# A sixth quad in the seven-product form in every MLP block of a two-layer decoder trunk

## What is computed

```python
def squared_relu_mlp(h, w_up, w_down):
    a = jnp.square(jax.nn.relu(h @ w_up))      # (256, 2048) @ (2048, 8192)
    return a @ w_down                          # (256, 8192) @ (8192, 2048)

for layer in range(2):
    x = x + mixer(rmsnorm(x, ln_mix_g[layer])) # attention of two kinds
    x = x + squared_relu_mlp(rmsnorm(x, ln_mlp_g[layer]), w_up[layer], w_down[layer])
```

## Time and profile before

| what | value |
|---|---|
| median of 3 runs | 2080.2 us |
| profiled execution, own time | 2079.74 us |
| its span, first to last instruction | 2078.0 us |
| TensorE busy | 2065.8 us |
| VectorE busy | 1451.2 us |
| ScalarE busy | 1087.7 us |
| granted clock of TensorE | 1.00 throughout |
| one MLP block, of 8 | 172.86 us |

### The profile page before, as it was taken

The page is one execution under the profiler, slowest core; times in us unless marked ns, Lnnn a source line. Parts: engine busy times, 40 slices in busy tenths (PEclk is TensorE's granted clock), DMA queues, the critical chain, the costliest instruction groups (busy, mean ns, idle before and its releaser), DMA issues.

```text
span 2078.0 us, 25877 instructions
## 1 busy us (share of the span) xinstructions
PE 2065.8 (99%) x10386; PEld 1751.5 (84%) x10386; DVE 1451.2 (70%) x1893; ACT 1087.7 (52%) x1553; POOL 85.5 (4%) x133
## 2 busy tenths in 40 slices
PE   8999999999999999999999999999999999999999
PEld 7888888888888888888888898888888888888887
DVE  6545555566966876886697687556886796687787
ACT  6545565445544544554556676444554454454454
POOL 0000000000000000000000255000000000000000
PEclk9999999999999999999999999999999999999999
DMA  8544554655566566565555443455565565656554
GB/s 285 175 151 163 162 162 143 193 174 191 195 199 202 175 225 187 174 223 179 193 193 184 156 127 122 162 182 182 182 223 182 196 204 187 198 184 209 181 182 162
DMA packets 198479, 381.96 MB, mean 184 GB/s; under 512 B 10892, under 2 KB 17112, under 8 KB 198360
## 3 DMA queue, kind: packets, MB, share of 16 engines
q1 hardware_dynamic: 198312, 380.29, 56.4%
q10 hardware_dynamic: 48, 0.02, 0.0%
HBM read 378.19 MB, written 2.10 MB: 183 GB/s over the span
## 4 chain that ended last, share of the span: by engine, by line
PE 98%; DVE 1%; ACT 0%; DMA 0%; issue 0%; POOL 0%; SPq 0%; DVEq 0%; ACTq 0%; POOLq 0%
PE psum L1505 23%; PE psum L1436 14%; PE psum L1438 14%; PE psum L1437 14%; PE psum L1508 11%; PE psum L1726 5%; PE psum L1727 5%; PE psum L1725 5%; PE psum L1569 1%; PE psum L1655 1%; PE psum L1523 1%; DVE halves L988 0%; PE psum L1632 0%; PE psum L1478 0%; PE psum L1656 0%; PE psum L1616 0%
## 5 line engine op out<-in xcount | busy, mean ns | idle before, releaser
L988 DVE TENSOR_TENSOR halves<-raw,halves 128x1024 fp32r<-128x1024 f32 (+1 forms) x724 | 858.0, 1194 | 461.0 <-ACT halves L696 455.9
L696 ACT CAST halves<-raw 128x1024 fp32r<-128x1024 f32 (+1 forms) x724 | 730.3, 1019 | 646.2 <-PE psum L1438 343.7
L1505 PE MATMUL psum<-h,halves 128*128 128x512 f32 x2048 | 639.2, 395 | 0.0
L1508 PEld LDWEIGHTS psum<-h,halves 128*128 128x128 f32 x2048 | 380.3, 188 | 87.4
L1508 PE MATMUL psum<-h,halves 128*128 128x256 f32 x2048 | 398.1, 278 | 0.0
L1436 PE MATMUL psum<-halves,a 128*128 128x512 f32 x828 | 326.3, 394 | 0.0
L1438 PE MATMUL psum<-halves,a 128*128 128x512 f32 x828 | 322.8, 390 | 0.0
L1437 PE MATMUL psum<-halves,a 128*128 128x512 f32 x828 | 322.4, 389 | 0.0
L1505 PEld LDWEIGHTS psum<-h,halves 128*128 128x128 f32 x2048 | 314.4, 189 | 2.8
L1436 PE MATMUL psum<-halves,h 128*128 128x512 f32 (+1 forms) x508 | 202.0, 398 | 0.0
L1438 PE MATMUL psum<-halves,h 128*128 128x512 f32 (+1 forms) x508 | 195.0, 384 | 0.0
(11 more groups left out here) (239 smaller groups left out, 1867.3 us busy)
## 6 DMA issues: line engine op xcount, KB each, us to landing
raw<-in_mlp_w_up SPq DMA_DIRECT2D x128, 1024.0 KB, 5.3
raw<-in_mlp_w_down SPq DMA_DIRECT2D x128, 1024.0 KB, 5.2
raw<-in_sf_w_in SPq DMA_DIRECT2D x45, 1024.0 KB, 5.1
raw<-in_sf_w_o SPq DMA_DIRECT2D x16, 1024.0 KB, 5.1
raw<-in_mla_w_o SPq DMA_DIRECT2D x16, 1024.0 KB, 5.1
raw<-in_mla_w_down SPq DMA_DIRECT2D x8, 1024.0 KB, 5.1
raw<-in_mla_w_ukv SPq DMA_DIRECT2D x8, 1024.0 KB, 5.4
raw<-in_mla_w_uq SPq DMA_DIRECT2D x8, 768.0 KB, 4.6
```

What stands on the lines that cost most here:

```text
L696: nc.scalar.copy(half_piece(n, 0), raw_piece(n)).then_inc(hi_done, 1)
L988: v.tensor_tensor(half_piece(n, 1), raw_piece(n), half_piece(n, 0).bitcast(F32), ALU.subtract)\
L1505: last = mm(bank, half_piece(n, 0)[:, cols], src[:, k].rearrange("p s t -> p (s t)"), start=(k == 0), stop=(k == KT - 1))
L1508: last = mm(bank[:, T:2 * T], half_piece(n, 1)[:, cols], src[:, k, 0], start=False, stop=False)
```

## The change

Quads 0, 1, 3, 4, 6 and 7 take the seven-product form in place of 0, 1, 3, 5 and 7; quads 2 and 5 stay plain. A block has 76 pieces in place of 75. The sixth set of token sums gets a buffer `sd_nat` in the memory of `nat`, which is the work buffer of the up projection; it is made while column 0 of the down projection runs. The places of all weight sums in the order of VectorE are set anew, and the counts in the waits follow (18 and 24 per block in place of 15 and 20).

```diff
-FAST_QUADS = 0, 1, 3, 5, 7
-PLAIN_QUADS = 2, 4, 6
+FAST_QUADS = 0, 1, 3, 4, 6, 7
+PLAIN_QUADS = 2, 5
...
+        with nc.sbuf_tensor("sd_nat", [P, 4, 2, P], F32R) as sd_nat:
+            pass
         nat = sb("nat", [P, 2, TT, N])
...
         def sd_of(i):
-            return sd[:, i] if i < 4 else sd_last[:]
+            return sd[:, i] if i < 4 else (sd_last, sd_nat)[i - 4][:]
...
                 for j in range(32, BLOCK_PIECES):
                     if base + j + AHEAD < P_END:
                         split_hi(base + j + AHEAD)
+                    if j == 34:
+                        token_sums_hi(no, 5)
...
-                sums = {35: 0, 37: 1, quad_at(2) - 3: 2, quad_at(4) - 3: 3, quad_at(6) - 3: 4}
+                sums = {34: 0, 37: 1, quad_at(2) - 3: 2, quad_at(3) - 1: 3, quad_at(5) - 2: 4, quad_at(6) - 1: 5}
...
                     if j == 33:
                         token_sums_lo(no, 4)
+                        token_sums(no, 5)
+                    if j == 35:
+                        token_sums_lo(no, 5)
```

More of the change, by code:

```diff
@@ L147, in all_pieces @@
             for i, (kind, load, half) in enumerate(block_plan(layer, b0)):
-                count = 15 * block_no(layer, b0) + 3 * load + (1 if kind == "t13" else 3) if kind[0] == "t" else 0
+                count = 18 * block_no(layer, b0) + 3 * load + (1 if kind == "t13" else 3) if kind[0] == "t" else 0
                 put(block_base(layer, b0) + i, kind, load, half, count)
@@ L933, in token_sums_hi @@
             def token_sums_hi(no, i):
-                act.wait_ge(a_step, 20 * no + 4 * i + 4)
+                act.wait_ge(a_step, 24 * no + 4 * i + 4)
                 nc.scalar.copy(sd_of(i)[:, :, 0], a_sum).then_inc(sd_hi, 1)
@@ L1274, in weight_sums @@
                 one, two = pair_loads(layer, b0, q // 2)
-                done = 15 * block_no(layer, b0) + 3 * m
+                done = 18 * block_no(layer, b0) + 3 * m
                 for load in (one, two):
@@ L1289, in token_sums @@
             def token_sums(no, i):
-                done = 20 * no + 4 * i
+                done = 24 * no + 4 * i
                 if done:
@@ L1303, in token_sums_lo @@
             def token_sums_lo(no, i):
-                dve.wait_ge(sd_hi, 5 * no + i + 1)
+                dve.wait_ge(sd_hi, 6 * no + i + 1)
                 v.tensor_tensor(sd_of(i)[:, :, 1], a_sum, sd_of(i)[:, :, 0].bitcast(F32), ALU.subtract)                 .then_inc(sd_ready, 1)
@@ L1788, in mlp_block @@
                             if q in FAST_QUADS:
-                                pe.wait_ge(sd_ready, 5 * no + FAST_QUADS.index(q) + 1)
+                                pe.wait_ge(sd_ready, 6 * no + FAST_QUADS.index(q) + 1)
                                 fast_quad(base + quad_at(q), q, added0 + 1)
```

## The result

The kernel after took **2100.97 us** (median of 4 runs, 2100.5 to 2103.26) beside 2080.26 of the kernel before on the same chip: ratio 1.0102, interval 1.0089 to 1.0114. It is slower by 20.7 us, where 15.2 were forecast. 1.0102 on the 2080.2 of the front is 2101.4, just above the range. The sign, the three places and their releasers came out as forecast. What failed is the price of a wait beyond its length: TensorE's start behind its releaser, forecast at 0.05 us, and its restart, forecast at nothing, each once per wait.

The account below looks back on a forecast made before the run. TensorE was taken to set the pace. Three stalls put on 2.58 us per block, the saving takes off 0.68: 1.90 net, 15.2 in eight blocks, so 2095.4 us against the median 2080.2; range 2089 to 2101, likeliest case 2093 to 2100.

Parts of the forecast that it names:

- the three places: TensorE would wait, per block, at the third piece of quad 0 and the first pieces of quads 4 and 7.
- the rival of the full saving: VectorE's average slack, 37 us per block, hides the added work; all 5.4 us show, 2074.8 us; chance 0.05.
- The saving: TensorE's matmuls for one more seven-product quad fall from 24 to 21: 0.68 us per block, 5.4 in all.
- Stall A: Third piece of quad 0 waits for VectorE's additions to x_tok, delayed by the sixth token sums: 0.97 us per block.
- B: First piece of quad 4 waits for VectorE's split, behind weight sums between quads 3 and 4: 0.68 us per block.
- C: First piece of quad 7 waits for VectorE's split, after two sets of weight sums: 0.93 us per block.
- A chain of 5.2: Between quads 3 and 4, TensorE's 4.76 us of work would have to hold a VectorE chain of 5.2.
- Unknown costs ... I take nothing, as that row is the nearest: TensorE's restart behind a 512-column matmul: nothing taken; upper bound 0.16 us per stall, 3.9 us in all.
- each stall costs more than its wait: Rival: twice the 0.16 us restart bound at each of 24 stalls, 7.7 us on top, 2103 us; chance 0.07.
- which changes nothing in this sum: Quad 0's weight sums, moved from j = 35 to 34, stay ahead of the additions: no effect on their delay.
- VectorE is the later one there: ScalarE's casts 39 and 40 are ready before VectorE asks, so ScalarE's added casts cost nothing.
- recorded 0.16 shorter than the loss: TensorE's waits in the profile after would read about 0.8, 0.5 and 0.8 us at the three places.

Follow-up runs that it names:

- work_free: The kernel after without the sixth token sums and the weight sums of quads 4 and 7: 2074.98 us, ratio 0.9974.
- no_token: The kernel after without the sixth token sums and ScalarE's cast of them, all weight sums kept: 2091.46 us, ratio 1.0055.
- no_sums_4: The kernel after without the weight sums of quad 4 alone: 2094.34 us, ratio 1.0068.
- no_sums_4_7: The kernel after without the weight sums of quads 4 and 7, sixth token sums kept: 2084.45 us, ratio 1.0019.
- token_only: The kernel before plus the sixth token sums, made but unused, weight sums of quad 0 still at j = 35: 2094.59 us, ratio 1.0069.
- token_only_34: token_only with the weight sums of quad 0 moved from j = 35 to j = 34: 2089.59 us, ratio 1.0042.
- delay_060: The kernel before plus one useless VectorE operation of 512 elements per block, ahead of the additions to x_tok: 2082.8 us, ratio 1.0014.
- delay_114: The kernel before plus one useless VectorE operation of 1024 elements per block, ahead of the additions to x_tok: 2087.31 us, ratio 1.0033.
- delay_228: The kernel before plus two useless VectorE operations of 1024 elements per block, ahead of the additions to x_tok: 2095.98 us, ratio 1.0073.
- respread: The kernel after with the three operations of each set of weight sums put behind splits of their own: 2084.88 us, ratio 1.0023.
- vector_sums: pool_sums with the weight sums of quads 2 and 3 back on VectorE, those of quads 0 and 1 one split earlier: 2101.81 us, ratio 1.0104.
- pool_sums: The kernel after with fast quads 0, 1, 2, 3, 5, 7, sixth token sums inside the up projection, weight sums of quads 2 and 3 on GpSimd: 2128.38 us, ratio 1.0229.

## Why the prediction was right, and where it was wrong

- **What bounds the kernel**: right. TensorE, with VectorE close behind it in the quads; the average slack of 37 us per block was of no use, although the rival of the full saving counted on it.
- **The saving**, 0.68 us per block: right, shown by work_free.
- **Stall A, B, C**: right in place, releaser and cause, shown by taking the causes away (A in no_token, B in no_sums_4, B and C in no_sums_4_7), and independent of each other. VectorE's lateness was 0.96, 0.64 and 0.94 for 0.92, 0.63 and 0.88. Two readings beside stall B were loose. "A chain of 5.2" is 5.4 by the prediction's own rows (4.76 + 0.68). And the b22 split is not held by piece 49 alone: its cast on ScalarE runs from 714.90 to 715.53, and the split starts at 715.70, directly behind the split before it. So something earlier could have helped, by some 0.13 us. Neither changes the sum.
- **"Unknown costs ... I take nothing, as that row is the nearest"**: this step failed, together with the 0.05 us for TensorE's start taken from the same. Both terms had the right place in the sum and the wrong size. A wait costs 0.15 before the first matmul and 0.08 to 0.12 in the steps behind it, 0.25 together, where I had 0.05: 0.20 x 24 = 4.8 of the 5.7 us that the rows show missing. Neither size was hidden. In the trace of before TensorE waits for another engine in the mixers too, and the earlier trace rows is only one of two kinds of start. The other, behind VectorE:

```profile
1180.45 0.74 DVE L1163 TENSOR_SCALAR mix<-psum,gains 128x512 f32<-128x512 f32 x1
...
1181.31 0.42 PEld L1569 LDWEIGHTS psum<-ident,mix 128*128 128x128 f32 x4 [0.93 <-issue]
1181.34 0.63 PE L1569 MATMUL psum<-ident,mix 128*128 128x128 f32 x4 [0.64 <-DVE mix L1163]
```

1180.45 + 0.74 = 1181.19, the weight load 0.12 behind it, the matmul 0.15. The three stalls wait for VectorE too, so this was the nearer row. The slow step behind a first matmul stands in that trace as well, at 512 columns, though behind small matmuls and not behind a wait:

```profile
177.04 0.47 PE L1436 MATMUL psum<-halves,h 128*128 128x512 f32 x1
177.35 0.39 PE L1437 MATMUL psum<-halves,h 128*128 128x512 f32 x1
```

A record of 0.47 and a step of 0.31, as behind all three stalls; the trace of before has 72 such pairs. With 0.15 and 0.08 in place of 0.05 and nothing the forecast would have been 0.18 x 24 = 4.3 us higher, 2099.7. By its own upper bound (0.16 for the restart, 3.8 us in all) it would have been 2099.2. And the range added this bound and the 2 us for the durations only in part: both on top of 2095.4 give 2101.3, where "2093 to 2100" stands.
- **The rival "each stall costs more than its wait"** is what came true, at two thirds of the 0.32 per stall that it was priced with. I gave it 0.07 and wrote that nothing in the rows shows it. The rows just shown were in the trace, outside the MLP.
- **The rest**, 0.11 us of lateness per block, 0.9 us in all: it lies within the 0.01 on each duration that the text allowed for. What makes it up was not taken apart.
- **"which changes nothing in this sum"**, of the weight sums of quad 0 moved from j = 35 to 34: the sum was right with them at 34, the sentence was not. With them at 35, and the quads of before, VectorE waits another 0.5 us for ScalarE (token_only, token_only_34), 4.9 us in all. I had costed ScalarE's new cast at nothing because "VectorE is the later one there"; that holds with the move and not without it. So this term of nothing came out right by luck.
- **"recorded 0.16 shorter than the loss"**: the waits read 0.94, 0.63 and 0.93 for losses of 1.21, 0.87 and 1.21, 0.24 to 0.28 shorter, as the steps behind a wait are slower too.

## What to carry to other kernels

- When a change puts work on an engine that feeds the bound one through a few buffers, follow each delivery from the step that frees its buffer to the step that needs it; the average slack says nothing. To every delivery that is late add the consumer's own restart, here 0.2 to 0.25 us, even if it is late by 0.04; and count as late what comes less than 0.15 us early.
- A consumer whose records overlap can lose time without showing idle time. Read the steps from start to start against the pace.
- The price of a wait can be read before any wait exists in the stretch of the change: search the whole trace for that engine waiting elsewhere, and take all kinds of restart that it shows, not one row.
- An idle engine is not free help. Before moving additions to GpSimd, look for VectorE's operations with two inputs in SBUF in the same stretch, and allow for TensorE's clock: here waits of up to 1.7 us left it at full speed, and each of 2.6 and 3.6 us was followed by a stretch at half.

## What the runs showed of the hardware that was not expected

- TensorE's surcharge behind a wait of 0.04 to 1.72 us is 0.24 to 0.26 us whatever its length (delay_060, delay_114, delay_228): the weight load starts 0.11 us after the releaser's end, the matmul 0.03 later, and the next step takes 0.31 in place of 0.227. Where weight load and matmul start together, 0.05 us behind the releaser, it is 0.2 us (respread, vector_sums).
- It begins before the wait does: a delivery 0.03 us early cost 0.2 us, one 0.11 us early 0.12 us (respread).
- In the MLP, waits of up to 1.7 us left the granted clock at 1.0. In pool_sums a wait of 3.6 us was followed by 5.65 us at 0.50, and all eight such waits (one of 2.6 us, seven of 3.6) by a stretch of matmuls at half speed.
- VectorE's addition of 512 elements took 2.77 us in place of 0.69 beside GpSimd's operations on the same memory, and ended 0.54 us after the one of GpSimd's that it had met.
